# An eleventh gather place from the third tile on, and the first head's query weights fetched with the others

## What is computed

```python
z = x @ w_in                              # q, k, v for attention, a and g for the conv group
att  = dilated sliding-window attention(q, k, v)
conv = silu(layer_norm(causal_conv_31(a * sigmoid(g))))
x1 = layer_norm(ALPHA * x + concat(att, conv) @ w_out)
# PEER: 8 heads; each picks 16 experts of 16384 for every row
q = (x1 @ w_query)                        # 8 heads x 2 sides x 128
s = q . sub_keys                          # 128 keys a side, top 16 of each, top 16 of the 256 sums
act  = gelu(x1 . expert_u[e])             # for the 128 chosen experts of a row
peer = sum_e gate[e] * act[e] * expert_v[e]
y = layer_norm(ALPHA * x1 + peer)
```

## Time and profile before

| | us |
|---|---|
| runs (3) | 3455.15, 3459.23, 3467.26 |
| median | 3459.23 |
| the profiled execution, its own time | 3465.34 |
| its span, first to last instruction | 3463.5 |
| moved by DMA | 1386.73 MB, mean 400 GB/s |
| busy: VectorE, TensorE, GpSimd, ScalarE | 2709.9, 2575.3, 1259.1, 718.4 |

### The profile page before, as it was taken

One profiled execution on the slowest core, in us unless ns is written; L12 is line 12 of the kernel. 1 busy time (PEld: TensorE's weight loads), 2 busy tenths in 40 slices (PEclk: granted clock), 3 DMA queues, 4 the chain that ended last, 5 costly groups with the idle time before them and its releaser, 6 DMA issues.

```text
span 3463.5 us, 39997 instructions
## 1 busy us (share of the span) xinstructions
PE 2575.3 (74%) x14040; PEld 1166.4 (34%) x14040; DVE 2709.9 (78%) x7309; ACT 718.4 (21%) x1565; POOL 1259.1 (36%) x1092
## 2 busy tenths in 40 slices
PE   6975588777767776777668767876787666789876
PEld 5544245322332333233324332433243322233321
DVE  5388788799799869996979699969996984345855
ACT  2210132023102310241005201520152002122100
POOL 0122123134434443444335444543444332224342
PEclk7998789888988897898788888998898888899999
DMA  9999899989999999999989999999999999999997
GB/s 334 383 409 416 347 390 367 424 318 421 421 412 365 421 421 421 395 416 421 420 343 399 421 421 398 417 421 421 392 416 421 421 408 422 419 419 398 417 390 329
DMA packets 218457, 1386.73 MB, mean 400 GB/s; under 512 B 28424, under 2 KB 39176, under 8 KB 67336
## 3 DMA queue, kind: packets, MB, share of 16 engines
q0 software_dynamic: 156672, 1140.92, 80.4%
q1 hardware_dynamic: 41040, 141.81, 10.7%
q10 hardware_dynamic: 20544, 101.45, 7.2%
HBM read 1370.99 MB, written 80.04 MB: 419 GB/s over the span
## 4 chain that ended last, share of the span: by engine, by line
DVE 38%; DMA 28%; PE 21%; issue 9%; ACT 2%; POOL 1%; SPq 0%; POOLq 0%; ACTq 0%; another core or an unknown queue 0%; DVEq 0%
DMA t<-in_expert_uv,t 26%; DVE t L1099 12%; PE psum L1477 10%; DVE t L966 4%; PE psum L1379 3%; PE psum L1420 3%; DVE psum L1126 2%; DMA t<-glu_scratch 2%; DVE t L1111 2%; DVE t L1047 2%; DVE t L1045 1%; DVE t L1048 1%; DVE t L1046 1%; DVE t L990 1%; PE psum L1301 1%
## 5 line engine op out<-in xcount | busy, mean ns | idle before, releaser
L645 POOL DMA_INDIRECT t<-in_expert_uv,t x1088 | 1258.9, 1157 | 2170.4 <-PE psum L1473 825.4
L1477 PE MATMUL psum<-t,t 64*64 64x512 f32 x4896 | 1356.6, 693 | 646.1 <-DVE t L1111 640.6
L1099 DVE CUSTOM_DVE_ANT_0 t<-t,t 128x1024 f32<-128x1024 f32 x1088 | 1322.9, 1222 | 462.5 <-DMA t<-in_expert_uv,t 441.7
L1477 PEld LDWEIGHTS psum<-t,t 64*64 64x64 f32 x4896 | 344.9, 149 | 1470.6 <-DVE t L1111 863.0
L1473 PE MATMUL psum<-t,t 64*64 64x512 f32 x2496 | 763.5, 741 | 0.0
L805 ACT ACTIVATE t<-t 128x2 f32<-128x2 f32 x544 | 110.8, 204 | 1851.5 <-DVE t L1099 1817.4
L1420 PEld LDWEIGHTS psum<-t,t 128*128 128x128 f32 x2304 | 274.1, 198 | 74.9 <-issue 66.8
L1301 PE MATMUL psum<-t,t 128*128 128x128 f32 (+2 forms) x768 | 257.1, 495 | 48.2 <-DMA t<-in_xT 41.7
L1420 PE MATMUL psum<-t,t 128*128 128x128 f32 (+1 forms) x2304 | 285.4, 284 | 2.6 <-ACT t L767 2.6
L966 DVE SCALAR_TENSOR_TENSOR t<-t,t,t 128x128 f32<-128x128 f32 x840 | 238.3, 346 | 0.0
L1301 PEld LDWEIGHTS psum<-t,t 128*128 128x128 f32 x768 | 132.0, 202 | 161.7 <-issue 118.5
(11 more groups left out here) (142 smaller groups left out, 2070.4 us busy)
## 6 DMA issues: line engine op xcount, KB each, us to landing
t<-in_wq_t ACTq DMA_DIRECT2D x65, 1024.0 KB
out<-in_cache_k_win SPq DMA_DIRECT2D x8, 4080.0 KB
out<-in_cache_v_win SPq DMA_DIRECT2D x8, 4080.0 KB
t<-in_w_in_t ACTq DMA_DIRECT2D x44, 512.0 KB, 11.4
t<-in_kc_t SPq DMA_DIRECT2D x8, 2560.0 KB
t<-in_vc_t SPq DMA_DIRECT2D x8, 2560.0 KB, 14.1
t<-in_expert_uv,t POOLq DMA_INDIRECT x1088
t<-in_w_v_t ACTq DMA_DIRECT2D x6, 1024.0 KB
```

Source lines behind the costliest of these rows:

```text
L645: pool.indirect_dma_start(ring[:, r, :], None, I["expert_uv"], bass.IndirectOffsetOnAxis(ap=idn[t % 2][:, s:s + 1], axis=0)).then_inc(land ...
L1099: dve.tensor_tensor_reduce(out=ring[:, r, 0:D], in0=x1[t % 2][:, :], in1=ring[:, r, 0:D], scale=1.0, scalar=0.0, op0=ALU.mult, op1=ALU.add ...
L1477: last = pe.matmul(MAIN[t][half][NS * a:NS * a + NS, :], zt[NS * a:NS * a + NS, k % Z_RING, j, :], vv[NS * a:NS * a + NS, :], start=(c == ...
```

## The change

The 8 KB a partition of `wq0` become an eleventh place of the ring, used from slot 0 of tile 2 on. From there gather k waits for the pair that holds slot k-11; the first one waits instead for what lay in this memory before. Head 0's weights are fetched for every tile with the other heads', and SP's single load of them goes.

```diff
+WIDE_FROM = 2 * SLOTS - FIRST_SLOTS
-        wq0 = at(o_l, [P, KD, 2 * KEYC])
+        last_place = at(o_l, [P, ROW])
-        landed = [sem(f"landed{i}") for i in range(RING)]
+        landed = [sem(f"landed{i}") for i in range(RING + 1)]
+        turn = [ORDER[k % RING] for k in range(WIDE_FROM)]
+        turn += [([RING] + turn[WIDE_FROM - RING:])[k % (RING + 1)] for k in range(TILES * SLOTS - FIRST_SLOTS - WIDE_FROM)]
+        seen = [FIRST_SLOTS // FIRST_RING if r in ORDER[0:FIRST_RING] else 0 for r in range(RING + 1)]
+        used = []
+        for r_ in turn:
+            used.append(seen[r_])
+            seen[r_] += 1
         def spot(t, s):
             k = t * SLOTS + s - FIRST_SLOTS
             if k < 0:
                 return ORDER[s % FIRST_RING], s // FIRST_RING
-            j = k % RING
-            return ORDER[j], (FIRST_SLOTS // FIRST_RING if j < FIRST_RING else 0) + k // RING
+            return turn[k], used[k]
+        def place_of(r):
+            return last_place[:, :] if r == RING else ring[:, r, :]
-        KEPT_FROM = 2
         def streamed(m):
-            return list(range(1 if m >= KEPT_FROM else 0, PH))
+            return list(range(PH))
-                if n == 1:
-                    sp.wait_ge(glus_kept, CT)
-                    sp.wait_ge(vs_out, 16)
-                    sp.dma_start(wq0[:, :, :], I["wq_t"][0]).then_inc(wq0_in, 16)
+                elif k == WIDE_FROM:
+                    pool.wait_ge(glus_kept, CT)
+                    pool.wait_ge(vs_out, 16)
+                    for i in range(3):
+                        pool.wait_ge(glu_out[i], GLU_ALL[i])
                 else:
-                    t_, s_ = divmod(k - RING + FIRST_SLOTS, SLOTS)
+                    t_, s_ = divmod(k - RING - (1 if k > WIDE_FROM else 0) + FIRST_SLOTS, SLOTS)
                     pool.wait_ge(pv, pair(t_, s_ // 2) + 1)
```

More of the change, by code:

```diff
@@ L348, in build @@
         ln_in = sem("ln_in")
-        wq0_in = sem("wq0_in")
         proj_done = sem("proj_done")
@@ L641, in gather @@
                             pool.wait_ge(q_out[i], 64)
+                elif k == WIDE_FROM:
[3 more added lines that the diff above has]
+                        pool.wait_ge(glu_out[i], GLU_ALL[i])
                 else:
-                    t_, s_ = divmod(k - RING + FIRST_SLOTS, SLOTS)
+                    t_, s_ = divmod(k - RING - (1 if k > WIDE_FROM else 0) + FIRST_SLOTS, SLOTS)
                     pool.wait_ge(pv, pair(t_, s_ // 2) + 1)
-                pool.indirect_dma_start(ring[:, r, :], None, I["expert_uv"],
+                pool.indirect_dma_start(place_of(r), None, I["expert_uv"],
                                         bass.IndirectOffsetOnAxis(ap=idn[t % 2][:, s:s + 1], axis=0)).then_inc(landed[r], 16)
@@ L1098, in dot @@
                     dve.wait_ge(x1_done, 2 * (t + 1))
-                dve.tensor_tensor_reduce(out=ring[:, r, 0:D], in0=x1[t % 2][:, :], in1=ring[:, r, 0:D], scale=1.0,
+                dve.tensor_tensor_reduce(out=place_of(r)[:, 0:D], in0=x1[t % 2][:, :], in1=place_of(r)[:, 0:D], scale=1.0,
                                          scalar=0.0, op0=ALU.mult, op1=ALU.add, accum_out=dots[t % 2][:, s:s + 1]).then_inc(a_dot, 1)
@@ L1414, in queries @@
                     w_ = wq[:, i, :, :]
-                else:
-                    pe.wait_ge(wq0_in, 16)
-                    w_ = wq0
                 for side in range(2):
@@ L1467, in values_pair @@
                         r, _ = spot(t, 2 * c + j)
-                        vv = ring[:, r, D + half * 512:D + (half + 1) * 512]
+                        vv = place_of(r)[:, D + half * 512:D + (half + 1) * 512]
                         if t == PT:
```

## The result

The changed kernel takes 3497.68 us (median of 6 runs, 3486.64 to 3504.39), the kernel before 3458.7 us in the same comparison (6 runs, 3451.85 to 3467.26): ratio 1.0112, interval 1.0095 to 1.013, so about 39 us or 1.1% slower. The forecast was 3503. The profiled execution took 3495.95 us, its span is 3494.1 us.

What follows compares the result with a forecast made beforehand. Tiles were taken as DMA-bound at 421 GB/s plus a little idle time. From the profiled 3465.3 us, weights +17.5, place -17.5 and three lost turns +37.5 gave 3503 us; likeliest case 3490 to 3516, with A 3458 to 3516.

Steps and rivals of the forecast that it cites:

- The turn: End of a step: one more queued gather makes the gl load take 24 us; 12.5 us each for tiles 3, 5, 6.
- one slow engine: Gl load ahead of tile 4: engines 7 and 15 usually slower; one would suffice, the load completing only with its last part.
- Its size: Turns ahead of tiles 3, 5 and 6: 12.5 us each, 37.5 us; bounds 0 to 12.5 a turn.
- The rule by which I chose tiles: Turns: next gather effectively 2.5 us earlier, at or under tile 4's 5.05 us after gl's issue, means a 24 us load.
- The place as buffer: VectorE's late stretch: an eleventh place gives back one gather, 2.5 us in each of tiles 2 to 8; bounds 0 to 2.5.
- rival D: Faster: weights' load costs nothing in VectorE's late stretch, place gives 2.5 us in each of seven tiles; 3448 us, chance 0.05.
- Weights: Steps 1 to 7: seven added loads of head 0's weights by ScalarE, 2.5 us of DMA each, 17.5 us.
- SP's load that went: SP's single load, issued at 732.25 us where DMA share is 0.63: removal worth 0 to 2.5 us, taken as 0.
- A: Rival: the turn isn't touched; weights +17.5, place -17.5; 3465 profiled, 3459 by the median, 3456 to 3472; chance 0.22.
- E: Rival: the place does nothing, only the weights show, +17.5 us; 3483 us, chance 0.08.
- B: Rival: the turn is touched cheaply or not everywhere, one or two turns, 12.5 to 25 us; 3475 to 3490, chance 0.10.
- C: Rival: all four turns are lost, tile 2's as well; 3515 us, chance 0.10.

Runs made afterwards that it cites:

- weights alone: Kernel before with ten places, all eight heads' weights fetched for every tile and head 0's single load removed: 3472.67 us against 3453.87, ratio 1.0055.
- one gather less: Changed kernel, but slot 4's gather in tiles 2 to 6 waits for the pair it would with ten places: 3465.32 us, ratio 1.0039.
- place alone: Changed kernel without head 0's weight fetches from tile 2 on, head 0 using head 1's weights: 3480.62 us, ratio 1.007 to the kernel before.

## Why the prediction was right

**The turn.** Forecast: with one more gather queued, gl takes some 24 us ahead of tiles 3, 5 and 6, as ahead of tile 4 before, and tile 2 is spared. In the profile: 22.3 us and more ahead of tiles 3, 4 and 5 (13.6 to 16.5 us of waiting), 15.3 us (7.0 of waiting) ahead of tile 6, tile 2 spared. Tiles of 360 us were forecast; 358, 358, 362 and 352 came. The cause is shown, not only fitting: taking the one gather away at five places gave 25 us back, and with it went every long load ahead of tiles 3 to 6. Why the late load is late I had put down to gathers beside it, with one slow engine as a second possibility; it was both, as the DMA records below show.

**Its size.** Forecast 37.5 us over the profiled execution of the kernel before, which had lost one turn already, so 43.6 over the median; measured 25. In the profile tiles 3 to 6 are 8, 8, 12 and 2 us longer than the 350 us of a tile with the weights alone, where 12.5 was forecast. Tile 6 was hit least, and the runs differ by 18 us (3486.64 to 3504.39), which I read as turns that are hit in some runs and not in others. I had said that with all turns lost the spread would go; it did not. The rule by which I chose tiles, 5.05 us from gl's issue to the next gather less 2.5 us, was too sharp: in the changed kernel tile 2 had 7.5 us between them and was spared, tile 3 had 7.9 and was hit.

**The place as buffer.** Forecast -2.5 us in each of seven tiles, -17.5. Measured between -5 and nothing: weights alone against one gather less, 1.0055 and 1.0039, with overlapping intervals, and nothing with gl on its own queue. This term was mis-sized. I had taken the whole idle time of a turn for want of a place, on the strength of its size being near 2.5 us. The row that I used against rival D spoke against this term too: at a share of 1.01 from 1110 to 1390 the late stretch of VectorE has no idle time for a place to give back. What was idle lay at the turn. That the next limit there, gathers released two by two by TensorE's pairs behind VectorE, was only a little further on is my guess; no run shows it. The bounds 0 and 2.5 us were right, the choice in them was not.

**Weights.** Forecast 17.5 us, measured 19, and 2.5 us a tile in the stretches. SP's load that went gave nothing back, as taken.

**The sum** was near by luck, by two errors that mostly cancel. Over the median it had 17.5 + 43.6 - 17.5 = 44 us; the runs have 19 + 25 - 5 = 39. So the turns were 18.6 us too dear and the place's gain 12.5 us too large. The 25 and the 5 are differences of the same three ratios and add up by themselves; the independent check is the place alone, 24 us, which with the weights' 19 gives 43 for 39.

**The rivals.** A (no turn touched), D (faster) and E (only weights) fell with the first trace, E once more with the place-alone run. B (one or two turns, 12.5 to 25 us) came near: against the profile before, which has tile 4 lost too, the profile after has lost two turns more and part of a third, and 25 us is the end of B's price. The median lies over B's 3490 because the place gave less than B took, too. C had tile 2 hit as well, which it was not. I had set A's time by taking the place's gain for the weights' price; turns left alone, the change costs 13 to 19 us, so A would have been slower too. Its range to 3472 was also too narrow for its own condition: with a place worth nothing it is 3459 + 17.5 = 3477 by the median.

**The page's rule.** I used the Trainium skill (DMA: Bandwidth & Descriptors, Queues, rings and completion order), taking turns at packet granularity, as if it made a small load quick. The runs show that the number of pieces counts: 22 to 25 us for both loads' pieces, 14 for half of them, 10 for a quarter. That fits a load fed in by turns against a standing queue.

How long a turn is, the DMA records in the traces show, which none of the views above print. The two loads are 1024 pieces, 64 for each of the 16 engines. Ahead of tile 4 before the change, 980 of them had started 9.5 us after gl's issue; the last 44 came one by one, 0.33 us apart, until 23.3 us. Ahead of tile 3 in the changed kernel it was the same: 980 within 9.6 us, the last 44 some 0.34 us apart, until 21.5 us. A gather's piece of 8 KB takes 0.31 us and a piece of the loads 0.03 us, so this is the pace of a single engine that moves one small piece for each piece of a gather (now and then two). The records carry no engine number; that it is one engine is read from this pace, and which one is not shown. Where the load was quick, ahead of tile 3 before, the last 44 came 0.03 us apart and the last one 11.2 us after gl's issue: in that time this engine, too, moved no gather pieces, so it had none.

So fifteen engines are done early in either case, and the extra gather decides only whether the last one runs empty. A turn here is one piece of each queue, not a packet of many descriptors; where the page and the measurement differ, the measurement decides. The sizes follow: some 3.5 us until the first piece starts, then 64 or 32 pieces at 0.34 us, is 25 and 14 us, for 22 to 25 and 13 to 15 measured.

## What to carry to other kernels

A buffer on a transfer-bound stream is not free where something small and urgent shares the transfer engines: what deepens the queue also delays the small load, and if the engine that frees the buffers waits for it, the stream stops. Look for the turn at which a short load is waited for, and see whether it gets in only because the stream pauses there. Put the load that is waited for first, or cut it into few large pieces, before adding depth: with eleven places either took the change from 3498 to 3472 us, though with ten places neither gained anything that can be measured. And don't value a place by the idle time seen: here 17.5 us were expected from it, and between nothing and some 5 came.

## What the runs showed of the hardware that was not expected

A 316 KB load behind a 256 KB one, both in pieces of about half a kilobyte, took 9 to 12 us where the gathers' queue ran empty and 22 to 25 us where it did not, though the DMA engines moved 429 GB/s in 9 of the last 11 us of such a load, more than the 421 of the quiet stretch. In the long load ahead of tile 4, all but 44 of the two loads' 1024 pieces had started after 9.5 us; the rest went through one late engine at one piece for each 8 KB piece of the gathers, 0.33 us apart. With the order swapped it took 14 us, in a quarter as many pieces 10 us. One gather (1 MB) more or less in the queue moved it from the one range to the other, with little in between: ahead of tiles 2 to 6 of the changed kernel only one load, 15.3 us, was neither short nor long.
